# Softmax sums of a hybrid attention block: one float32r product with ones in place of two bf16 products

## The reference

```python
q = einsum(rmsnorm(c_q), w_uq)      # 16 heads, 128 + 64 rotary
kv = einsum(rmsnorm(c_kv), w_ukv)   # 16 heads, 128 for k, 128 for v
sc = einsum('bqhd,bkhd->bhqk', q_full, k_full) * ATTN_SCALE
sc = where(key_chunk <= q_chunk, sc, -inf)      # chunks of 64
p = softmax(sc)
attn = einsum('bhqk,bkhd->bqhd', p, v)
y_attn = attn * silu(z_attn)
```

## Time and profile before

| | us |
|---|---|
| median of 3 runs | 2633.36 |
| lowest and highest of them | 2598.59, 2702.06 |
| the profiled execution | 2598.04 |
| span of its slowest core (core 4) | 2596.4 |
| spans of cores 0 to 3 | 2596.1, 2564.6, 2566.6, 2568.7 |
| spans of cores 4 to 7 | 2596.4, 2564.1, 2564.8, 2573.5 |

### The profile page before, as it was taken

How to read it: one execution, slowest core, us unless ns; L and a number is a source line. 1 busy time by engine, 2 the same in 40 slices (tenths; PEclk the granted TensorE clock), 3 DMA queues, 4 the chain that set the end, 5 groups by cost and what they waited for, 6 DMA issues and landing times.

```text
span 2596.4 us, 37267 instructions; the slowest of 8 cores (2564.1 to 2596.4 us)
## 1 busy us (share of the span) xinstructions
PE 2472.4 (95%) x14487; PEld 1397.7 (54%) x14630; DVE 1259.5 (49%) x1953; ACT 410.6 (16%) x739; POOL 59.6 (2%) x110
## 2 busy tenths in 40 slices
PE   6889999999999999999999999988888899999997
PEld 3445555555555555555555555545444466665443
DVE  4768666444544455443336332677777511115214
ACT  2110000000000000001011001444444300001012
POOL 0000000000000000000000000111110000000000
PEclk8999999999999999999999999999999999999999
DMA  7753444444444444420344443999971344448966
GB/s 173 175 133 108 153 140 142 136 145 147 144 151 153 153 153 144 135 82 16 129 130 128 126 124 86 168 148 138 127 141 33 113 140 142 157 140 245 344 212 212
DMA packets 126652, 374.17 MB, mean 144 GB/s; under 512 B 13568, under 2 KB 19072, under 8 KB 126336
## 3 DMA queue, kind: packets, MB, share of 16 engines
q1 hardware_dynamic: 106976, 311.18, 38.8%
q0 software_dynamic: 17184, 56.25, 14.0%
q10 hardware_dynamic: 2304, 4.20, 0.4%
HBM read 402.59 MB, written 58.79 MB: 178 GB/s over the span
## 4 chain that ended last, share of the span: by engine, by line
PE 89%; DVE 4%; ACT 3%; issue 3%; DMA 1%; ACTq 0%; DVEq 0%; POOLq 0%; POOL 0%; SPq 0%
PE ps L678 33%; PE ps L1166 12%; PE ps L918 9%; PE ps L1353 7%; PE ps L620 6%; PE ps L898 5%; PE ps L977 4%; PE ps L794 3%; PE ps L1250 2%; PE ps L997 1%; PE ps L987 1%; PE ps L1068 1%; PE ps L1067 1%; PE ps L600 1%; ACT rl_a L1088 1%
## 5 line engine op out<-in xcount | busy, mean ns | idle before, releaser
L678 PE MATMUL ps<-XG_a,ws_a 128*128 128x360 bf16 (+2 forms) x4940 | 865.0, 337 | 2.7
L678 PEld LDWEIGHTS ps<-XG_a,ws_a 128*128 128x128 bf16 x4992 | 488.5, 98 | 379.0
L449 DVE TENSOR_TENSOR ws_a<-stg_a,g_in_a 128x1024 bf16<-128x1024 f32 x304 | 358.3, 1220 | 166.4 <-DMA stg_a<-w_in_t 166.3
L918 PE MATMUL ps<-XG_a,ws_a 128*128 128x360 bf16 (+1 forms) x1521 | 266.4, 337 | 1.4 <-DVE zt_a L936 0.6
L918 PEld LDWEIGHTS ps<-XG_a,ws_a 128*128 128x128 bf16 x1536 | 150.2, 98 | 117.1 <-issue 0.7
L620 PE MATMUL ps<-XG_a,uw_a 128*128 128x360 bf16 (+1 forms) x944 | 177.6, 349 | 18.8 <-DVE Pz_a L523 7.7
L1166 PE MATMUL ps<-YA_a,WO_a 128*128 128x360 bf16 x1024 | 160.2, 317 | 0.0
L1166 PE MATMUL ps<-G_a,WO_a 128*128 128x360 bf16 x1024 | 159.3, 316 | 0.0
L620 PEld LDWEIGHTS ps<-XG_a,uw_a 128*128 128x128 bf16 x960 | 96.3, 101 | 99.4 <-issue 29.7
L977 PE MATMUL ps<-CQG_a,WQ_a 128*128 128x360 bf16 (+1 forms) x765 | 144.3, 337 | 0.7
L898 PE MATMUL ps<-XG_a,ws_a 128*128 128x360 bf16 (+1 forms) x767 | 137.0, 337 | 0.4
(11 more groups left out here) (158 smaller groups left out, 2051.7 us busy)
## 6 DMA issues: line engine op xcount, KB each, us to landing
stg_a<-w_in_t SPq DMA_DIRECT2D x304, 512.0 KB, 5.0
WO_a<-wbf SPq DMA_DIRECT2D x128, 512.0 KB, 4.4
wbf<-w_out_t POOLq DMA_DIRECT2D x64, 512.0 KB, 18.9
ust_a<-w_in_t SPq DMA_DIRECT2D x36, 512.0 KB, 5.2
XA_a<-x_own SPq DMA_DIRECT2D x32, 360.0 KB, 4.2
outA<-HA_a SPq DMA_DIRECT2D x32, 360.0 KB, 11.2
XG_a<-x_own POOLq DMA_DIRECT2D x15, 616.0 KB, 8.9
wst_a<-w_ckv SPq DMA_DIRECT2D x16, 576.0 KB, 5.0
```

The lines of the kernel that those rows point to most:

```text
L449: tt(WS[i % 2][:, 8 * c:8 * c + 8, :], stg[q % 3][:, :, :], gains(8, 8 * c, 128), ALU.mult)
L678: mm(o, w[:, kc, :], XG[:, kc, c0:c1], kc == 0, kc == 31)
L918: mm(o, w[:, kc, :], xk(kc, g), kc == 0, kc == 31)
```

## The change

`ls` is written as float32r (4 bytes, the same region as before); the cast and the subtraction are gone, and one product takes `ls` whole against a matrix of ones in float32r, `onesr`, which one copy on VectorE makes ahead of the attention stage. The list of a closing block has five operations in place of seven, and `spread` is written anew for five. The `for _ in range(3)` after the loop of steps is not touched.

```diff
--- before.py
+++ after.py
@@ -945,10 +945,9 @@
     TQ = [zsb(az, "TQ%d" % i, [n], BF16) for i in range(2)]
     PT = [zsb(az, "PT%d" % i, [2, 512], BF16) for i in range(4)]
     ACC = [zsb(az, "ACC%d" % i, [2, 512]) for i in range(2)]
-    ls = zsb(az, "ls", [512])
+    ls = zsb(az, "ls", [512], F32R)
     rl = zsb(az, "rl", [512])
-    lhi = zsb(az, "lhi", [512], BF16)
-    llo = zsb(az, "llo", [512], BF16)
+    onesr = zsb(az, "onesr", [128], F32R)
     WQ = [sb("WQ%d" % i, Z_R + (16 + 8 * i) * KB, [8, 256], BF16) for i in range(2)]
     WKV = [sb("WKV%d" % i, Z_R + (20 - 20 * i) * KB, [4, 512], BF16) for i in range(2)]
     free = az.left()
@@ -1001,6 +1000,7 @@
         while evq:
             evq.pop(0)()
 
+    cp(onesr[:, :], ones16[:, :])
     load_wq(0)
     load_wkv(0)
     load_wq(1)
@@ -1076,21 +1076,18 @@
         w = b - a
         o = []
         g_ = G[:, h, a:b]
-        ls_, lhi_, llo_, rl_ = ls[:, 0:w], lhi[:, 0:w], llo[:, 0:w], rl[:, 0:w]
+        ls_, rl_ = ls[:, 0:w], rl[:, 0:w]
 
         def sums():
             b_ = ubank() if sumbank[0] is None else sumbank[0]
             o.append(psum[:, b_, 0:w])
-            mm(o[0], ones16[:, :], lhi_, True, False)
-            mm(o[0], ones16[:, :], llo_, False, True)
+            mm(o[0], onesr[:, :], ls_, True, True)
 
         def inverse():
             act(rl_, o[0], AF.Ln)
             act(rl_, rl_, AF.Exp, scale=-1.0)
 
         return [lambda: tt(ls_, A[:, 0, 0:w], A[:, 1, 0:w], ALU.add),
-                lambda: cp(lhi_, ls_),
-                lambda: tt(llo_, ls_, lhi_, ALU.subtract),
                 sums, inverse,
                 lambda: tt(rl_, rl_, g_, ALU.mult),
                 lambda: tt(g_, psum[:, 4 + gb % 2, 0:w], rl_, ALU.mult)]
@@ -1177,7 +1174,7 @@
 
     def spread(x):
         c = sum(1 for q in per if q[0] == per[(x + 1) % SP_][0])
-        return (range(7) if c > 6 else (0, 0, 1, 2, 2, 3, 4) if c > 4 else (0, 0, 1, 2, 2, 3, 3) if c > 3 else (0, 0, 0, 1, 1, 2, 2))
+        return (0, 1, 2, 3, 4) if c > 4 else (0, 1, 1, 2, 3) if c > 3 else (0, 1, 1, 2, 2)
 
     NS = len(steps)
     WCE = max(1, int(NS * 0.85) // 64)
```

## The result

The changed kernel takes 2573.03 us (median of 5 runs; 2565.11 to 2573.70 in those that count), against 2598.59 us before (median of 5 runs taken beside them; 2595.91 to 2598.59 in those that count). Left out are one of the five, at 3053 us, which ran with a granted clock of 0.81 on one die, and the runs of 2633 and 2702 us of the kernel before. The forecast was 2569 us and 1.1%.

The account below looks back on a forecast made before the run. Place 0 (core 4, 2596.4 us) bounded the kernel; its terms gave 2546.6, so place 3 would bound at 2573.5 - 5.8 = 2567.7. With 1.6 us from span to run time the forecast was 2569 us, range 2556 to 2640.

Parts of the forecast that it names:

- Which place bounds: Whole kernel: place 0 falls from 2596.4 to 2546.6 us, so place 3, at 2567.7, becomes the bound.
- the sum for place 0: Core 4's end: 2596.4 - 8.3 - 15.0 - 1.1 - 27.0 + 1.6 = 2546.6 us.
- The products: Closing sums: one float32r product for two bf16, columns streamed once; saves 8.3 us in place 0, 5.8 in place 3.
- The VectorE work: Without cast and subtraction the TQ evacuation frees the sums' bank earlier; place 0 saves 15.0 us plus 1.1 at line 1085.
- The order: Sums a step earlier exchange PSUM banks; V and K unit waits go, 27.0 us in place 0; places 1 to 3: 0.
- The wait on line 1096: Place 0's 17.6 us of TensorE waiting for a block's gated output stay; worth 0.
- The end of the stage: After the loop the product waits 2.6 us for `ls`, where 1.0 was waited; costs 1.6 us in place 0, 0 in place 3.
- The rest: Copy for `onesr` 0, or 0.4 us uncovered; buffers shrink 1.5 KB; no DMA added or moved, WQ loads pulled forward.
- The total: Whole kernel: 2569 us, 1.1% below the profiled run's 2598.0, with place 3 as the bound.
- The terms of place 3: Core 7's end: products save 5.8 us, order 0 with 2 us either way, end of stage 0; 2573.5 becomes 2567.7.

Follow-up runs that it names:

- the pair of experiments that differs in the product: Kernel before with the new steps, against changed kernel with cast and subtraction put back; attention stage 388.3 against 380.0 us (place 0), 826.6 against 821.8 (place 3).

## Why the prediction was right, step by step

- *Which place bounds.* Right. Place 0 was to end at 2547 and ended at 2552 and 2555; place 3 sets the time. This step made the forecast, not the sum for place 0.
- *The products.* Right in kind, columns once: 8.3 and 5.8 us were worked out for places 0 and 3; the pair of experiments that differs in the product gives 8.3 and 4.8. The agreement in place 0 is luck in part: the listed waits alone fell by 6.8 us there, and the clock took some 1.7 back. The 190 ns load shows at most as the 0.05 us by which the product of 512 columns exceeds its columns.
- *The VectorE work.* The releaser was inferred rightly (a bank held by the TQ unit), the size not: 16.1 us taken, 8.7 net. The term went wrong by assuming that what follows moves along unchanged; the chain to the gated output and WQ took some of it back.
- *The order.* 27.0 us for place 0 taken; 27.4 measured with the order alone in the kernel before, 21.4 in the changed kernel, and by the estimate without the clock's share 25.7 and 23.1. The exchange of banks shows in the timeline. For places 1 to 3 I wrote 0 with 2 us either way; it is -4.3 or -7.1 in place 1, +1.1 or -0.1 in place 2, -1.8 or -3.8 in place 3 (first in the kernel before, then in the changed one), outside those 2 us in place 1 and, in the changed kernel, in place 3. The missed mechanism is ScalarE's: with sums and inverse at the later steps, the exponentials were waited for more (5.4 against 0.9 us in place 3 with the order alone changed, 7.5 against 1.5 in the changed kernel).
- *The wait on line 1096.* Said to stay; 17.6 us became 19.4.
- *The end of the stage.* 2.6 us of wait expected in place 0, 2.5 measured; from the last score product to the end core 4 takes 551.7 us against 549.2, 2.5 more where 1.6 were expected, within what this stretch varies between traces.
- *The rest.* "No DMA is added or moved" was true and yet missed a cost: the same casts in a shorter head fill the DMA engines, and WQ goes from 10.4 to 29.1 us, twice too late for TensorE. The stage of place 0 is 7.0 us longer than the sum said (371.3 against 415.7 - 8.3 - 15.0 - 1.1 - 27.0 = 364.3), which is the same 7 us that the VectorE term lacks; spreading the casts brings 363.0, some of it by the clock.
- *The total.* 2569 against 2573.0. The terms of place 3 came to 5.8 where its stage lost 6.7, for a partly different reason: 4.8 of product and about 2 of order. The rest of the distance is the start of the stage, which moves by some us from run to run: in the four runs that count the last core of place 3 ends at 2571.5, 2565.6, 2572.1 and 2563.6 us, 2568.2 on the mean, beside the 2567.7 of the sum. That it comes so close is luck in part, since two errors of the terms cancel and single runs lie up to 5 us from the mean.

## What to carry to other kernels

When several programs run side by side, work the change out for each and take the maximum: here 44 us off the slowest were worth 25. Where buffers are handed out in turn, a closing operation moved by one step changes which wait every later user inherits; it can be worth more (21 to 27 us of place 0's stage here) than the instruction that was saved (8 us), and it can be had without it. A stage that gets shorter needs its background DMAs spread anew, or they return as waits of the loads beside them.

## What the runs showed of the hardware

- A float32r product of 464 or 384 columns passes its columns once at full rate: 0.186 us each for a mean of 425 columns (place 3, four products in place of one), 0.200 for 471 (place 2). Its 128 x 128 weight load takes 190 ns, against 98 ns for a bf16 load, and hides behind the columns but for some 0.01 us.
- Plain fp32 shows as two instructions and took 0.79 us for 464 columns, four times the columns' time.
- After 3.15 us of waiting, TensorE's next 16 products of 360 columns took 4.27 us in place of 2.60, at a granted clock of 0.72 over the window; after 2.66 us of the same waiting in another kernel they took 2.60. The same wait of 2.50 us in the last head was followed by a clock of 0.57 over 4 us in one kernel and of 1.00 in the other. So in these traces the length of a wait alone does not tell whether the clock falls.
- Five casting DMAs of 512 KB per head of some 23 us filled the DMA engines (share 1.01 from 1640 to 1900 us), and a 512 KB load on the same queue landed after 29.1 us; with 4.3 casts per head (share 0.91) it landed after 8.0.
